# Prompt heads of a hybrid decoder step: values stationary and two heads to a product, dilated scores in pairs, no turn of the head outputs

## The chip, the cores and the metric

One core of one Trainium2 chip. The time is the device time of one execution in microseconds (us); less is better. The shapes are fixed: 256 prompt tokens, 8 sample tokens, 2 layers.

## What is computed

Each layer adds to the residual stream a mixer (latent attention, dilated-window attention and a convolution, side by side, through one output projection), and then a large expert layer (PEER). The change is in the mixer's attention over the 256 prompt tokens and in how its result reaches the output projection.

```python
for l in range(DEPTH):                                   # 2 layers
    hn = rmsnorm(xp, norm_mix[l])
    ...                                                  # project_in: queries, latents, dilated q, k, v, conv gate
    a_out = mla_prompt(q_nope, q_rope, c_kv, k_r, w_ukv[l])          # 6 heads of 64
    b_out = combine_dilations([dilated_prompt(qb, kb, vb, wdw, dl) for wdw, dl in DIL_PATTERNS], xp.dtype)  # 6 heads of 64
    c_out = conv_module(g_ext, conv_w[l], conv_b[l], conv_ln_g[l], conv_ln_b[l])                             # 256 channels
    xp = xp + jnp.concatenate([a_out, b_out, c_out], axis=-1) @ w_out[l]
    ...                                                  # PEER over 16,384 experts
```

For each head: scores of 256 queries against the keys, a mask, a softmax, and the product with the values. The 8 sample tokens have attention of their own, over 2,048 cached positions each.

## The kernel before

The kernel is written engine by engine; each engine runs its list in order, and semaphores tie them. Three of its habits matter here.

**The step loop.** After the input projection every engine walks the same loop, `for s in range(2 * NH + 2)`, 14 steps for 12 heads (0 to 5 latent, 6 to 11 dilated), L1078 for TensorE, L1447 for ScalarE, L1983 for VectorE. Head s is scored in step s (`scores`, L980: for latent heads two products of 128 and of 32 contracted rows for each half of the queries, for dilated heads one product with 64 contracted rows, L992). VectorE adds the mask, finds the maximum and writes `prob` (L1988). ScalarE takes the exponential and its sum (L1461). In step s+1 TensorE turns the three 128x128 blocks (`turn_probs`, "PT"), ScalarE copies them to `probT` (L1465). In step s+2 `mix_values` (L999, "O") takes the turned probabilities as the stationary operand and the 64 value columns as the moving one: three products of 64 columns. VectorE divides the result by the sum into `oAB`, tokens on the partitions (L2002, L2005).

Between them, in the same steps, goes the sample tokens' attention: for sequence b, in the steps of PAST_STEP = (0, 1, 2, 3, 5, 6, 8, 9), `turn_past` turns 16 + 4 blocks (banks "cT" and "rT"), which ScalarE copies out (L1454, L1456; the one `cT` buffer may be written only after sequence b-1 has been scored); one step later `score_past` ("SC", L1027, L1030), after which VectorE finds its maximum (`past_max`, L1862) and ScalarE its exponential (L1472); one step later the turn of its probabilities ("PP"), and one more the product with the cache ("ol", L1043). Steps 4 and 7 score the windows of the sample tokens ("ws", L1053), step 11 multiplies them with their values ("ow", L1073, L1075). VectorE also does the convolution: five taps in each of steps 0 to 6 (L1807), the samples' part in step 8 (L1943), its statistics in step 10 (`conv_stats`, L1954).

**Eight PSUM banks in turn.** A table of jobs, `job_plan` (L88), names every product that goes to a bank and who empties it ("V" VectorE, "A" ScalarE); job n takes bank n mod 8, and TensorE begins a job only when the bank's previous job has been emptied:

```python
PRIOR = [max([m for m in range(n) if BANK[m] == BANK[n]], default=None) for n in range(len(JOBS))]
...
if PRIOR[n] is not None:
    wait_moved(pe, *JOBS[PRIOR[n]][0])
```

So the place of a job in the table sets whom it waits for.

**The tail.** After the loop TensorE turns `oAB` to channels on partitions (L1132, "mT", six jobs of two blocks), ScalarE rounds each to a high part in `hiT` (L1514), VectorE subtracts for the low part (L2028). Then the samples' output ("os", L1137), the turn of the convolution ("ycT"), its sigmoid on ScalarE (L1517) and its product and split on VectorE (`conv_out`, L1974 to L1980). `out_high` (L1153) multiplies the high and low parts with the high part of W_out, `out_low` (L1159) the high part with its low part; of its eight blocks of rows, the last two need the convolution. ScalarE casts W_out's first half (`out_weights_high(0)`, L1509) after the loop. SyncE loads W_out's second half after the last "ol" and right behind it the first block of the query weights (L588, L669); ScalarE casts the query weights (L1523) before the second half of W_out.

## Time and profile before

| | us |
|---|---|
| median of 3 runs (2064.66 to 2067.21) | 2066.34 |
| the profiled execution, its own time | 2067.32 |
| its span, first to last instruction | 2065.4 |
| TensorE busy | 2043.7 (99%) |
| VectorE busy | 1557.4 (75%) |
| ScalarE busy | 1300.2 (63%) |
| mean DMA rate | 233 GB/s |

The span falls into two layers of about 1030 us. In each the mixer takes the first 220 us or so, the PEER layer the rest. The step loop of the second layer runs from 1115 to 1209 us. The chain that ended last is 96% TensorE, most of it the PEER products L1226 and L1273, which the change does not touch. A busy TensorE is not TensorE at its peak: weight loads that nothing hides count as busy.

### The profile page before, as it was taken

How to read it: one execution, taken by the hardware profiler on the slowest of the kernel's cores; microseconds unless marked ns; L12 is line 12 of the kernel's file. 1: busy time of each engine (PE TensorE's matmuls, PEld its weight loads, DVE VectorE, ACT ScalarE, POOL GpSimd, SP SyncE). 2: the span in 40 equal slices, each digit the busy share in tenths (PEclk: the TensorE clock that was granted, in tenths of full speed). 3: DMA queues.
4: the chain of work that ended last, by engine and by line, in shares of the span. 5: the costliest groups of instructions: out<-in, count | busy, mean ns of one | idle time of the engine just before them, and what ended most of it. 6: DMA issues, size and time to landing. Idle time of an engine off the chain costs nothing.

```text
span 2065.4 us, 40864 instructions
## 1 busy us (share of the span) xinstructions
PE 2043.7 (99%) x15610; PEld 1805.3 (87%) x15610; DVE 1557.4 (75%) x3543; ACT 1300.2 (63%) x2567; POOL 118.9 (6%) x138
## 2 busy tenths in 40 slices
PE   9999999999999999999999999999999999999998
PEld 7777899999999888788887769999999998887887
DVE  6855789868899776676677466999688997766766
ACT  5466445658888655565564564556688876655654
POOL 2200010000000010100022000000000001101000
PEclk9999999999999999999999999999999999999999
DMA  9453447776666898898763543677766668988886
GB/s 324 145 162 134 162 153 254 248 252 221 208 220 220 282 314 284 302 322 281 248 228 142 171 164 124 200 252 252 241 220 215 214 218 300 317 287 293 267 268 221
DMA packets 137377, 481.78 MB, mean 233 GB/s; under 512 B 25666, under 2 KB 42082, under 8 KB 130768
## 3 DMA queue, kind: packets, MB, share of 16 engines
q1 hardware_dynamic: 124640, 438.45, 63.6%
q0 software_dynamic: 10496, 40.42, 5.6%
q8 instruction: 126, 2.06, 0.4%
q10 hardware_dynamic: 2048, 0.30, 0.1%
q14 instruction: 67, 0.55, 0.1%
HBM read 475.83 MB, written 104.21 MB: 281 GB/s over the span
## 4 chain that ended last, share of the span: by engine, by line
PE 96%; DVE 2%; ACT 1%; DMA 1%; issue 0%; DVEq 0%; ACTq 0%
PE ps L1226 36%; PE ps L1273 33%; PE ps L842 4%; PE ps L930 3%; PE ps L1238 3%; PE ps L1189 2%; PE ps L938 2%; PE ps L1197 2%; PE ps L1193 1%; PE ps L886 1%; PE ps L1153 1%; PE ps L1027 1%; PE ps L1212 1%; PE ps L895 1%; PE ps L1030 1%; DMA big<-in_peer_wq 1%
## 5 line engine op out<-in xcount | busy, mean ns | idle before, releaser
L2220 DVE TENSOR_TENSOR parts<-region,parts 128x1024 fp32r<-128x1024 f32 x512 | 625.7, 1222 | 300.6 <-ACT parts L1548 298.3
L1226 PE MATMUL ps<-tokens_hi,parts 128*128 128x256 f32 x4096 | 760.5, 284 | 0.0
L1548 ACT CAST parts<-region 128x1024 fp32r<-128x1024 f32 x512 | 538.7, 1052 | 271.1 <-PE ps L1273 207.5
L1273 PE MATMUL ps<-parts,parts_hw 128*128 128x512 f32 x3024 | 688.7, 390 | 0.0
L1273 PEld LDWEIGHTS ps<-parts,parts_hw 128*128 128x128 f32 x3024 | 567.0, 188 | 123.8 <-DVE parts_hw L2270 6.9
L1226 PEld LDWEIGHTS ps<-tokens_hi,parts 128*128 128x128 f32 x4096 | 636.9, 188 | 1.0 <-issue 0.6
L1226 PE MATMUL ps<-parts_hw,parts 128*128 128x256 f32 x2048 | 574.1, 280 | 0.0
L1226 PEld LDWEIGHTS ps<-parts_hw,parts 128*128 128x128 f32 x2048 | 386.8, 189 | 0.0
L1594 ACT ACTIVATE big<-ps 128x256 f32<-128x256 f32 (+31 forms) x252 | 131.7, 522 | 146.9 <-PE ps L1226 146.9
L1582 ACT CAST parts_hw<-big 128x256 fp32r<-128x256 f32 x256 | 170.6, 666 | 0.7 <-DVE big L2281 0.7
L1575 ACT ACTIVATE region<-region 128x128 f16<-128x128 f16 x512 | 169.3, 436 | 0.0
L2270 DVE TENSOR_TENSOR parts_hw<-big,parts_hw 128x256 fp32r<-128x256 f32 x256 | 158.5, 619 | 6.7 <-ACT parts_hw L1582 6.7
L1238 PE MATMUL ps<-region 128*128 128x128 f16 x1024 | 81.3, 220 | 0.0
L1592 ACT ACTIVATE big<-ps 128x256 f32<-128x256 f32 (+42 forms) x130 | 36.5, 281 | 67.1 <-PE ps L1226 67.1
L811 POOL DMA_INDIRECT region<-in_peer_u,eidx x16 | 17.9, 1116 | 875.0 <-PE ps L1273 746.4
L842 PE MATMUL ps<-ident,big 128*128 128x128 f32 (+4 forms) x446 | 66.3, 277 | 0.2
L1454 ACT COPY region<-ps 128x512 f32<-128x512 f32 x64 | 32.9, 601 | 51.5 <-PE ps L1030 35.0
L1238 PEld LDWEIGHTS ps<-region 128*128 128x128 f16 x1024 | 59.0, 97 | 5.6
L842 PEld LDWEIGHTS ps<-ident,big 128*128 128x128 f32 (+4 forms) x446 | 49.8, 143 | 13.7 <-issue 10.9
L2281 DVE TENSOR_TENSOR big<-big 128x256 f32<-128x256 f32 (+42 forms) x130 | 58.5, 450 | 1.6 <-ACT big L1592 1.3
L2244 DVE TENSOR_TENSOR region<-big,region 128x512 f16<-128x512 f16 x128 | 53.4, 417 | 0.0
L2251 DVE TENSOR_TENSOR region<-region 128x512 f16<-128x512 f16 x128 | 53.4, 417 | 0.0
(328 smaller groups left out, 2244.8 us busy)
## 6 DMA issues: line engine op xcount, KB each, us to landing
region<-in_peer_uT SPq DMA_DIRECT2D x256, 512.0 KB, 4.0
region<-in_peer_v SPq DMA_DIRECT2D x256, 512.0 KB, 4.8
out<-in_state_win_k SPq DMA_DIRECT2D x112, 384.0 KB, 4.8
out<-in_state_win_v SPq DMA_DIRECT2D x112, 384.0 KB, 5.0
big<-in_window_keysT SPq DMA_DIRECT2D x16, 576.0 KB, 5.5
big<-in_state_win_v SPq DMA_DIRECT2D x48, 192.0 KB, 4.5
region<-in_w_out SPq DMA_DIRECT2D x4, 2048.0 KB, 9.0
big<-in_peer_wq SPq DMA_DIRECT2D x4, 2048.0 KB, 11.1
```

The source lines that it names most:

```text
L842: mm = pe.transpose(o[0:cols, c0:c0 + rows], src, ident[0:rows, 0:rows])
L930: mm = pe.matmul(o[t][:, 0:n], part[:, k, 128 * t:128 * t + 128], w, start=(k == 0 and i == 0), stop=False, skip_group_check=True)
L1226: mm = pe.matmul(ps[:, j % ZB, 0:SEQ], a, hp[b][:, c, :], start=(c == 0 and n == 0), stop=(c == KD - 1 and n == 2))
L1238: mm = pe.matmul(ps[:, 4 + g % GBK, 128 * k:128 * k + 128], hotA[g % 2][:, k // 2, :, k % 2], hot[g % 2][:, k // 2, :, k % 2], start=(n == ...
L1273: mm = pe.matmul(ps[:, 2 * half + t, :], w_t[a][:, 128 * t:128 * t + 128], v_t[b][:, 512 * half:512 * half + 512], start=(j == 0 and n == ...
L1548: act.copy(hi_t[n % HIGHS], rows_t[n % ROWS]).then_inc(high[l], 1)
L1575: e = act.activation(hotC[g % 2][:, k // 2, :, k % 2], place_b[g % 2][:, k // 2, :, k % 2], ACT.Copy, scale=w14[:, GG * g + k:GG * g + k + 1])
L1582: act.copy(w_parts_of(j)[0], G[:, j // JH, :, j % JH]).then_inc(w_high[now[0]], 1)
L1594: e = act.activation(G[:, j // JH, done:SEQ, j % JH], z_o[:, done:SEQ], ACT.Gelu)
L2220: dve.tensor_tensor(lo_t[n % ROWS], rows_t[n % ROWS], hi_t[n % HIGHS], ALU.subtract).then_inc(low[l], 1)
L2270: dve.tensor_tensor(w_t[1], G[:, j // JH, :, j % JH], w_t[0], ALU.subtract).then_inc(w_ready[now[0]], 1)
L2281: dve.tensor_tensor(a, a, act_t[j % 2][:, 0:done], ALU.mult).then_inc(w_mul, 1)
```

## The change

The heads are mixed in pairs. The values are now the stationary operand (64 columns of each head, head 2g into partitions 0 to 63 of the bank and head 2g+1 into 64 to 127), the turned probabilities the moving one (256 and 128 columns), so that the output has channels on its partitions and needs no turn. The division by the sum can then no longer follow the product, where the sum would lie along the free axis; VectorE divides the probabilities themselves before they are turned (`divide`), and `turn_probs` waits for that. The pair's high part is copied by ScalarE (`high_heads`) and its low part formed by VectorE (`low_heads`) in the odd steps from 3 on. Both dilated heads of a pair are scored in the even step, their products alternating between contracted rows 0 to 63 and 64 to 127. ScalarE casts W_out's first half in step 11. The bank table changes with the jobs.

```diff
@@ -85,6 +85,12 @@
 
+def scored_in(s):
+    if s < NH:
+        return [s]
+    return [s, s + 1] if s < 2 * NH and s % 2 == 0 else []
...
@@ -103,19 +109,18 @@
-        if s < 2 * NH:
-            jobs.append((("S", s), "V"))
+        jobs += [(("S", u), "V") for u in scored_in(s)]
         if s == EXT_STEP:
             jobs.append((("ext",), "V"))
         if s in PAST_STEP:
             b = PAST_STEP.index(s)
             jobs += [(("cT", b, g), "A") for g in range(4)] + [(("rT", b), "A")]
+        if s >= 3 and s % 2:
+            jobs.append((("O", (s - 3) // 2), "V"))
         if 1 <= s <= 2 * NH:
             jobs.append((("PT", s - 1), "A"))
         if s - 1 in PAST_STEP:
             jobs.append((("SC", PAST_STEP.index(s - 1)), "A"))
-        if s >= 2:
-            jobs.append((("O", s - 2), "V"))
         if s - 2 in PAST_STEP:
             jobs.append((("PP", PAST_STEP.index(s - 2)), "A"))
         if s - 3 in PAST_STEP:
@@ -134,7 +139,6 @@
-    jobs += [(("mT", g), "V") for g in range(2 * HP)]
...
@@ -152,7 +156,19 @@
-BANK = [LATE.get(name, (n if n < NUM["mT", 0] else n + 6) % 8) for n, (name, _) in enumerate(JOBS)]
+OUT_BANK = [(NUM["xo", 0, t] + 2) % 8 for t in range(2)]
+BESIDE_OUT = [b for b in range(8) if b not in OUT_BANK]
+
+
+def bank_of(n, name):
+    if name in LATE:
+        return LATE[name]
+    if NUM["PT", 2 * NH - 1] <= n < NUM["xo", 0, 0]:
+        return BESIDE_OUT[(n - NUM["PT", 2 * NH - 1]) % 6]
+    return (n if n < NUM["os",] else n + 2) % 8
+
+
+BANK = [bank_of(n, name) for n, (name, _) in enumerate(JOBS)]
 PRIOR = [max([m for m in range(n) if BANK[m] == BANK[n]], default=None) for n in range(len(JOBS))]
...
@@ -977,35 +1005,42 @@
 
-                def scores(u):
-                    o = begin("S", u)
-                    h = u % NH
+                def latent_scores(h):
+                    o = begin("S", h)
+                    r0 = 32 * (h % 4)
                     for i, c0 in ((0, 0), (1, 128)):
                         K = 128 * (i + 1)
                         qs = slice(128 * i, 128 * i + 128)
-                        if u < NH:
-                            r0 = 32 * (h % 4)
-                            pe.matmul(o[:, c0:c0 + K], qlT[:, h, qs], ckvT[:, 0:K], start=True, stop=False)
-                            mm = pe.matmul(o[:, c0:c0 + K], qrT[r0:r0 + 32, h // 4, qs], krT[r0:r0 + 32, 0:K], start=False, stop=True)
-                        else:
-                            r0 = 64 * (h % 2)
-                            mm = pe.matmul(o[:, c0:c0 + K], qbT[r0:r0 + 64, h // 2, qs], kbT[r0:r0 + 64, h // 2, 0:K], start=True, stop=True)
+                        pe.matmul(o[:, c0:c0 + K], qlT[:, h, qs], ckvT[:, 0:K], start=True, stop=False)
+                        mm = pe.matmul(o[:, c0:c0 + K], qrT[r0:r0 + 32, h // 4, qs], krT[r0:r0 + 32, 0:K], start=False, stop=True)
                     mm.then_inc(product[now[0]], 1)
 
+                def dilated_scores(g):
+                    o = [begin("S", NH + 2 * g + n) for n in range(2)]
+                    for i, c0 in ((0, 0), (1, 128)):
+                        K = 128 * (i + 1)
+                        for n in range(2):
+                            r = slice(64 * n, 64 * n + 64)
+                            mm = pe.matmul(o[n][:, c0:c0 + K], qbT[r, g, 128 * i:128 * i + 128], kbT[r, g, 0:K], start=True, stop=True)
+                            if i:
+                                mm.then_inc(product[now[0]], 1)
+
                 def turn_probs(u):
-                    pe.wait_ge(exp_ready, u + 1)
+                    pe.wait_ge(prob_ready, u + 1)
                     turn("PT", u, parts=[(prob[:, u % 2, 128 * i:128 * i + 128], 128, 128, 128 * i) for i in range(3)])
 
-                def mix_values(u):
-                    wait_moved(pe, "PT", u)
-                    if u == 0:
+                def mix_values(g):
+                    wait_moved(pe, "PT", 2 * g + 1)
+                    if g == 0:
                         wait_moved(pe, "va", 1)
-                    o = begin("O", u)
-                    v = [va[:, t, 64 * u:64 * u + 64] if u < NH else z[:, t, VB + 64 * (u - NH):VB + 64 * (u - NH) + 64] for t in range(2)]
-                    pt = probT[:, u % 2, :]
-                    pe.matmul(o[:, 0:64], pt[:, 0:128], v[0], start=True, stop=True)
-                    pe.matmul(o[:, 64:128], pt[:, 128:256], v[0], start=True, stop=False)
-                    pe.matmul(o[:, 64:128], pt[:, 256:384], v[1], start=False, stop=True).then_inc(product[now[0]], 1)
+                    o = begin("O", g)
+                    for k, (q0, q1, p0) in enumerate(((0, 256, 0), (128, 256, 256))):
+                        for n in range(2):
+                            u = 2 * g + n
+                            v = va[:, k, 64 * u:64 * u + 64] if u < NH else z[:, k, VB + 64 * (u - NH):VB + 64 * (u - NH) + 64]
+                            mm = pe.matmul(o[64 * n:64 * n + 64, q0:q1], v, probT[:, n, p0:p0 + q1 - q0], start=(k == 0), stop=(k == 1),
+                                           skip_group_check=True)
+                    mm.then_inc(product[now[0]], 1)
 
...
@@ -1075,21 +1110,33 @@
                 for s in range(2 * NH + 2):
-                    if s < 2 * NH:
-                        scores(s)
+                    if s < NH:
+                        latent_scores(s)
+                    elif scored_in(s):
+                        dilated_scores((s - NH) // 2)
                     if s == EXT_STEP:
                         o = begin("ext")
                         pe.matmul(o[0:NB, 0:48], ckvT[:, SEQ:T], qlS[:, :, 0:NH], start=True, stop=False)
                         pe.matmul(o[0:NB, 0:48], krT[0:32, SEQ:T], qrB[0:32, :, 0, :], start=False, stop=True).then_inc(product[now[0]], 1)
                     if s in PAST_STEP:
                         turn_past(PAST_STEP.index(s))
+                    if s >= 3 and s % 2:
+                        mix_values((s - 3) // 2)
                     if 1 <= s <= 2 * NH:
                         turn_probs(s - 1)
                     if s - 1 in PAST_STEP:
                         score_past(PAST_STEP.index(s - 1))
-                    if s >= 2:
-                        mix_values(s - 2)
...
@@ -1127,9 +1174,6 @@
-                wait_moved(pe, "O", 2 * NH - 1)
-                for g in range(2 * HP):
-                    turn("mT", g, parts=[(oAB[:, t, 128 * g:128 * g + 128], 128, 128, 128 * t) for t in range(2)])
...
@@ -1444,6 +1478,15 @@
+                    act.wait_ge(w_ld[now[0]][(5 + c) % 2], 16 * ((5 + c) // 2))
+                    for k in range(KD):
+                        act.copy(out_high_part(c, k), wview(5 + c)[:, k, :]).then_inc(wo_high, 1)
+
+                def high_heads(g):
+                    o = arrive(act, "O", g)
+                    act.copy(mix_hi(g), o[:, 0:SEQ]).then_inc(mix_high, 1)
+
                 for s in range(2 * NH + 2):
...
@@ -1463,6 +1506,8 @@
+                    if s >= 3 and s % 2:
+                        high_heads((s - 3) // 2)
...
@@ -1493,6 +1538,8 @@
+                        act.wait_ge(product[now[0]], NUM["S", 2 * NH - 1] + 1)
+                        out_weights_high(0)
...
@@ -1503,15 +1550,6 @@
-                def out_weights_high(c):
-                    act.wait_ge(w_ld[now[0]][(5 + c) % 2], 16 * ((5 + c) // 2))
-                    for k in range(KD):
-                        act.copy(out_high_part(c, k), wview(5 + c)[:, k, :]).then_inc(wo_high, 1)
-
-                out_weights_high(0)
-                for g in range(2 * HP):
-                    o = arrive(act, "mT", g)
-                    act.copy(hiT[:, g, 0:SEQ], o[:, 0:SEQ]).then_inc(mix_high, 1)
...
@@ -1975,14 +2013,32 @@
+                def divide(u):
+                    dve.wait_ge(exp_ready, u + 1)
+                    step(dve.reciprocal(rden[:, u, :], den[:, u, :]))
+                    settle()
+                    for i, c0 in ((0, 0), (1, 128)):
+                        pr_ = prob[:, u % 2, c0:c0 + 128 * (i + 1)]
+                        e = dve.tensor_scalar(pr_, pr_, rden[:, u, i:i + 1], None, ALU.mult)
+                    e.then_inc(prob_ready, 1)
+
+                def low_heads(g):
+                    o = read("O", g)
+                    if g == 0:
+                        dve.wait_ge(stored, 1)
+                    dve.wait_ge(mix_high, g + 1)
+                    dve.tensor_tensor(mix_lo(g), o[:, 0:SEQ], mix_hi(g), ALU.subtract).then_inc(moved_v[now[0]], 1)
 
                 for s in range(2 * NH + 2):
                     if s < 2 * NH:
                         o = read("S", s)
+                        if s >= NH and s % 2:
+                            dve.wait_ge(product[now[0]], NUM["PT", s - 2] + 1)
                         for i, c0 in ((0, 0), (1, 128)):
                             c1 = c0 + 128 * (i + 1)
                             e = dve.tensor_tensor_reduce(prob[:, s % 2, c0:c1], o[:, c0:c1], (mbias if s < NH else cbias)[:, c0:c1],
@@ -1991,19 +2047,15 @@
                         settle()
                     if s == EXT_STEP:
                         new_scores()
+                    if 1 <= s <= 2 * NH:
+                        divide(s - 1)
                     some_taps(TAPS[s] if s < len(TAPS) else 0)
                     if s - 1 in PAST_STEP:
                         past_max(PAST_STEP.index(s - 1))
                     if s == 2:
                         window_queries()
-                    u = s - 2
-                    if u >= 0:
-                        dve.wait_ge(exp_ready, u + 1)
-                        step(dve.reciprocal(rden[:, u, :], den[:, u, :]))
-                        o = read("O", u)
...
@@ -2022,10 +2074,6 @@
-                for g in range(2 * HP):
-                    o = read("mT", g)
-                    dve.wait_ge(mix_high, g + 1)
-                    dve.tensor_tensor(mix_lo[:, g, 0:SEQ], o[:, 0:SEQ], hiT[:, g, 0:SEQ], ALU.subtract).then_inc(moved_v[now[0]], 1)
```

The places where high and low parts lie change too (`mix_hi`, `mix_lo`: the high parts of the heads in the room of `oAB`, the low parts in dead columns of `z` and `va`), which is why the first `low_heads` waits for `stored`.

How the order of instructions moves, at two places. TensorE, steps 6 to 7, from the product with the cache of the sequence before on (L1043 before, L1078 now). Names: `ps` is PSUM; `region` holds the rope part and the probabilities, `ident` is the identity of a turn. Before:

```order
L1043 MATMUL ps<-big 32x128 x16
L992 MATMUL ps<-big 128x128
L992 MATMUL ps<-big 128x256
L842 MATMUL ps<-ident,region 128x128 x16
L842 MATMUL ps<-ident,big 128x128 x4
L842 MATMUL ps<-ident,region 128x128 x3
L1027 MATMUL ps<-region,big 32x512 x4
L1030 MATMUL ps<-big,region 6x128 x16
L1006 MATMUL ps<-big,region 128x64
L1007 MATMUL ps<-big,region 128x64
L1008 MATMUL ps<-big,region 128x64
L1043 MATMUL ps<-big 32x128 x16
```

And now:

```order
L1078 MATMUL ps<-big 32x128 x16
L1024 MATMUL ps<-big 128x128 x2
L1024 MATMUL ps<-big 128x256 x2
L870 MATMUL ps<-ident,region 128x128 x16
L870 MATMUL ps<-ident,big 128x128 x4
L870 MATMUL ps<-ident,region 128x128 x3
L1062 MATMUL ps<-region,big 32x512 x4
L1065 MATMUL ps<-big,region 6x128 x16
L1078 MATMUL ps<-big 32x128 x16
L870 MATMUL ps<-ident,big 128x128 x3
L870 MATMUL ps<-ident,big 8x128
L1041 MATMUL ps<-region,big 64x256 x2
```

Two heads are scored at once, and the mix of a head between "SC" and "ol" is gone; the pair's mix opens step 7. "ol" of sequence 3 stands right behind "SC" of sequence 4, and its bank was that of the scores of head 7.

VectorE, steps 10 to 11, from the end of `past_max` on (L1864 before, L1902 now); `nmx` is the negative maximum, `den` the sum. Before:

```order
L1864 TENSOR_SCALAR big<-big 128x1
L2002 RECIPROCAL rden<-den 128x2
L2005 TENSOR_TENSOR big<-ps,rden 128x2x64
L1954 BN_STATS bnst<-big 128x6
...
L1958 TENSOR_SCALAR stat<-bnst 8x1
L1988 ISA region,nmx<-ps,big 128x128
L1988 ISA nmx 128x1
L1988 ISA region,nmx<-ps,big 128x256
L1988 ISA nmx 128x1
L2002 RECIPROCAL rden<-den 128x2
L2005 TENSOR_TENSOR big<-ps,rden 128x2x64
```

And now:

```order
L1902 TENSOR_SCALAR big<-big 128x1
L1992 BN_STATS bnst<-big 128x6
...
L1996 TENSOR_SCALAR stat<-bnst 8x1
L2044 ISA region,nmx<-ps,big 128x128
L2044 ISA nmx 128x1
L2044 ISA region,nmx<-ps,big 128x256
L2044 ISA nmx 128x1
L2023 RECIPROCAL rden<-den 128x2
L2027 TENSOR_SCALAR region<-region,rden 128x128
L2027 TENSOR_SCALAR region<-region,rden 128x256
L2035 TENSOR_TENSOR big_r<-ps,big_r 128x256
```

The rows L2027 are new: the division of head 10, which its turn on TensorE waits for, stands behind `conv_stats` and the maximum of head 11.

## Rows read from the trace of the kernel before

**Rows 1.** Windows, second layer: stretch, busy us of PE, PEld, DVE, ACT, POOL; then clock, DMA, GB/s.

```profile
1115.00:1243.00 128.00, 123.57 (x1414) 90.20 (x1413) 73.54 (x226) 76.03 (x195) 3.91 (x4) 1.00 0.45 153
```

**Rows 2.** Waits of TensorE, 1115 to 1245 us: us in total, times, longest.

```profile
PE ps L1153 <- DVE big_r L1980: 1.8, 1, 1.8
...
PE ps L992 <- ACT region L1465: 0.8, 1, 0.8
```

**Rows 3.** Timeline of TensorE, second layer: start us, us, instruction, [idle before].

```profile
1127.92 2.40 PE L842 MATMUL ps<-ident,big 128*128 128x128 f32 x20
...
1182.86 1.06 PE L1027 MATMUL ps<-region,big 128*32 128x512 f32 x8
...
1184.73 0.43 PE L1006 MATMUL ps<-big,region 128*128 128x64 f32 x2
...
1185.65 1.08 PE L1043 MATMUL ps<-region,big 128*32 128x128 f32 x32
...
1188.75 0.92 PE L992 MATMUL ps<-big 64*128 64x128 f32 x4 [0.78 <-ACT region L1465]
1189.60 0.55 PE L842 MATMUL ps<-ident,region 128*128 128x128 f32 x3
...
1196.91 2.14 PE L1073 MATMUL ps<-big 128*32 128x384 f32 x24
1198.99 0.91 PE L1075 MATMUL ps<-big 8*128 8x384 f32 x2
...
1208.78 1.75 PE L842 MATMUL ps<-ident,big 128*128 128x128 f32 x12
...
1217.05 0.47 PE L1153 MATMUL ps<-big_r,tokens_hi 128*128 128x512 f32 x1 [1.75 <-DVE big_r L1980]
...
1225.61 3.68 PE L895 MATMUL ps<-region,big 128*8 128x128 f32 x128
```

**Rows 4.** Groups by shape, TensorE, 1099 to 1115.1 us: count, busy us, mean ns, idle.

```profile
L886 PE MATMUL ps<-big 128*128 128x288 f32 x16 | 4.2, 413 | 0.7 <-DMA big<-in_w_ukT 0.7
...
L886 PE MATMUL ps<-big 64*128 64x264 f32 x12 | 1.6, 400 | 0.0
```

**Rows 5.** Timeline of VectorE, second layer.

```profile
1173.94 0.56 DVE L1883 COPY big<-ps 128x384 f32<-128x384 f32 x1 [2.11 <-PE ps L1057]
...
1175.38 0.28 DVE L1988 CUSTOM_DVE_ANT_0 region<-ps,big 128x128 f32<-128x128 f32 x1
...
1178.21 0.41 DVE L1943 TENSOR_TENSOR region<-region 128x248 f32<-128x248 f32 x1
...
1180.55 0.29 DVE L1988 CUSTOM_DVE_ANT_0 region<-ps,big 128x128 f32<-128x128 f32 x1 [0.18 <-DVE region L1947]
...
1193.42 0.42 DVE L1954 BATCH_NORM_STATS2 bnst<-big 128x6 f32<-128x256 f32 x1
...
1195.87 0.29 DVE L1988 CUSTOM_DVE_ANT_0 region<-ps,big 128x128 f32<-128x128 f32 x1 [0.18 <-DVE stat L1958]
...
1196.42 0.16 DVE L2002 RECIPROCAL rden<-den 128x2 f32<-128x2 f32 x1
...
1206.48 1.05 DVE L1967 TENSOR_SCALAR big<-big,bnst,stat 128x256 f32<-128x256 f32 x3
...
1209.99 2.08 DVE L2028 TENSOR_TENSOR big_r<-ps,tokens_hi 128x256 fp32r<-128x256 f32 x6 [0.83 <-ACT tokens_hi L1514]
```

**Rows 6.** Timeline of ScalarE, second layer.

```profile
1184.92 2.05 ACT L1454 COPY region<-ps 128x512 f32<-128x512 f32 x4 [4.56 <-PE ps L1030]
...
1188.20 0.50 ACT L1465 COPY region<-ps 128x384 f32<-128x384 f32 x1
...
1211.28 1.28 ACT L1517 ACT_TABLE_LOAD   x1
```

**Rows 7.** Chain of waits, 1030 to 1300 us: start us, us, what.

```profile
1205.39 14.15 DMA big<-in_peer_wq
```

**Rows 8.** Windows, first layer, columns as in rows 1.

```profile
182.00:194.00 12.00, 12.00 (x59) 9.77 (x58) 7.95 (x22) 7.36 (x15) 0.00 (x0) 0.57 0.92 342
```

More of the change, by code:

```diff
@@ L1076, in mix_window, with out_high @@
                               skip_group_check=True).then_inc(product[now[0]], 1)
+                def out_high(c, t, k0, k1):
+                    o = begin("xo", c, t) if k0 == 0 else bank("xo", c, t)
+                    for k in range(k0, k1):
+                        pe.wait_ge(wo_high, KD * c + k + 1)
+                        if c == 0 and k == 2 * HP:
+                            wait_moved(pe, "ycT", 1)
+                        for i, part in enumerate((mix_hi(k), mix_lo(k))):
+                            pe.matmul(o[:, 0:512], part[:, 128 * t:128 * t + 128], out_high_part(c, k), start=(k == 0 and i == 0), stop=False,
+                                      skip_group_check=True)
                 for s in range(2 * NH + 2):
-                    if s < 2 * NH:
-                        scores(s)
+                    if s < NH:
+                        latent_scores(s)
+                    elif scored_in(s):
+                        dilated_scores((s - NH) // 2)
                     if s == EXT_STEP:
@@ L1142, in _ @@
                     turn("ycT", c, parts=tokens(yt, 128 * c))
-                wait_moved(pe, "mT", 5)
                 wait_moved(pe, "os")
-                def out_high(c, t):
-                    o = begin("xo", c, t)
-                    for k in range(KD):
-                        pe.wait_ge(wo_high, KD * c + k + 1)
-                        if c == 0 and k == 2 * HP:
-                            wait_moved(pe, "ycT", 1)
-                        for i, part in enumerate((hiT, mix_lo)):
-                            pe.matmul(o[:, 0:512], part[:, k, 128 * t:128 * t + 128], out_high_part(c, k), start=(k == 0 and i == 0), stop=False,
-                                      skip_group_check=True)
+                wait_moved(pe, "O", 2 * HP - 1)
                 def out_low(c, t):
@@ L1998, in _ @@
                         window_queries()
[L1999 to L2006 removed]
+                    if s >= 3 and s % 2:
+                        low_heads((s - 3) // 2)
                     if s in WINDOW_STEP:
```

31 lines of the change are left out of this document (19 added, 12 removed).

## The prediction, made before the changed kernel ran

> **What bounds the kernel now.** I read the page's chain first: 96% TensorE, nearly all of it PEER, which stays as it is. So only the mixer counts, some 125 us of each layer. Then the windows over it: TensorE is busy 123.57 of 128 us, VectorE 73.54 and ScalarE 76.03 [rows 1]. In the step loop TensorE leads and the others keep up; its waits there are 0.8 us on ScalarE in step 10, and 1.8 us in the tail for the convolution's low part [rows 2]. Work taken off TensorE in the loop is therefore worth its full time, but only as long as the two other engines deliver in time: each of them is idle because TensorE is late, and their chains have latencies which a shorter TensorE step uncovers. So I price the work first and then look for every place where TensorE would arrive early. Times are those of the second layer; the first has the same sequence. T is the end of the sample scores "SC" of sequence 6, 1184.73 us [rows 3].
>
> **TensorE's work.** Mix: a head takes 0.92 us from its start to the next instruction (1184.73 to 1185.65) [rows 3]; over the 12 heads these spans run from 0.61 to 0.92 and add up to 9.2. Now a pair has 256 + 128 moving columns for each head, in two column halves. If the halves run side by side, that is 384 columns. A product of 288 columns on all rows takes 4.2/8 = 0.52 us, so 384 take 0.69; that column strips do run side by side is seen in the window mix, where 12 products of 384 columns in four strips need 2.08 us, 0.17 each [rows 3, 4]. With entry and exit I take 0.9 for a pair (ends 0.7 and, not side by side, 1.5): 9.2 - 5.4 = **3.8 saved**. Dilated scores: a head takes 0.85 (1188.75 to 1189.60) [rows 3]. Products with 64 contracted rows that alternate between the row halves are there already: six of 264 columns in 1.6 us, 0.27 each, where one on all rows takes 0.52 for 288 [rows 4]. So a pair costs about what a head did, 0.9 (ends 0.8 and 1.7): 5.1 - 2.7 = **2.4 saved**. The turns "mT" go: **1.7 saved** [rows 3]. Together 7.9 us of each layer.
>
> **VectorE's work.** The division of 128 outputs becomes one of 384 probabilities. Nearest row: a tensor by scalar of 256 elements, 0.35 us (three in 1.05); with the reciprocal's 0.27 and 0.1 to 0.2 for the 128-element part, **0.7 us a head** [rows 5]. Over the loop it adds little to an engine that idles 40% of the time. What it changes is the order: the division of head s-1 stands behind the maximum of head s (0.6 us, 1195.87 to 1196.42 and a little [rows 5]), and TensorE's turn PT(s-1) waits for it. Before, that turn needed ScalarE alone. In steps that open with 2.4 us of past turns (20 blocks, [rows 3]) this is hidden; in the others it is not.
>
> **Where TensorE now waits, up to T.** (a) "ol" of step 3 takes the bank of cT(3,1), which ScalarE empties 1.1 us after "SC"; "PP" covers 0.5: 0.6. (b) Step 4 has no past turns: from the end of S(4) VectorE needs 0.6 for the maximum, 0.7 for the new token's scores and 0.7 to divide, TensorE has one small product: 1.9 until PT(3). (c) Step 6: "ol" now has the bank of S(7), and VectorE comes to S(7) only after the maximum of "SC" (0.9), a small reciprocal (0.2) and 0.6 of its own; TensorE has nothing between: 1.8. (d) Step 8: "ol" has the bank of S(9). From the end of the window scores VectorE needs 1.4 (window maximum), 0.6, 0.7, 2.3 (samples' convolution) and 0.6 = 5.6; TensorE 0.9 + 2.4 + 0.4 + 0.5 = 4.2: 1.4, say 1.5 [rows 5, 3]. Sum 5.8. Up to T seven heads become four pairs (5.4 to 3.6) and four dilated heads two pairs (3.4 to 1.8): -3.4. **T comes 2.4 us later.**
>
> **From T to the window mix**, before 12.2 us (1184.73 to 1196.91 [rows 3]). S(10) now has the bank of O(3), the pair that was just mixed. ScalarE empties the four "cT", "rT", takes an exponential and copies PT(8), until T+4.0 (1188.70 [rows 6]), then the high part, and VectorE the low part, 0.35 each (2.08/6 [rows 5]): S(10) starts at T+4.8, where TensorE is ready at 3.0. The pair ends at 5.7, maximum and division at 7.1, PT(9) 7.6, "SC" (1.87) 9.5. Then VectorE takes its maximum (10.4), **`conv_stats`, 2.4 us** (12.8), the maximum of head 11 and the division of head 10: 14.1. TensorE has mixed a pair meanwhile and waits 3 us, the longest new wait. PT(10), "PP", "ol" (1.0) and one turn: 16.3. **4.1 us later.**
>
> **From there to the output projection's second part** (before 20.1 us, 1196.91 to 1217.05). Two single mixes (1.5) become a pair (0.9), behind 0.3 of wait: ScalarE's eight casts of W_out, 4.3 us, now stand ahead of the copies of the window mix, but the mix of the second group covers them except for 1 us, and TensorE has PT(11) and "ol" then. Without "mT" 1.7 go, less 0.3 which the copy for "os" then shows. ScalarE's table load before the sigmoid (1.28 us from 1211.28 [rows 6]) no longer stands behind "mT": 1.0. **2.7 us earlier.** From here on all is as before: `out_low` ends 8.6 us later (1225.61 [rows 3]).
>
> Off the path: the query weights' transfer is issued behind the last "ol" and lands after 14.15 us [rows 7]. "ol" ends at T+23.5 instead of T+20, so the weights land at T+38; ScalarE's casts (3.9 + 4.3) end at 46.3, VectorE gets there at 47.6. It stays hidden by 1.3 us; one more microsecond of delay would show. `stored` is set long before step 3 (the stores land in 10 us, some 15 us earlier).
>
> **Sum.** +2.4 + 4.1 - 2.7 = +3.8 us a layer, 7.6 for both. The profiled execution took 2067.3, 1.0 above the median of the runs: 2066.3 + 7.6 = **2074 us**. Differences of less than 0.2%, 4.1 us, count as none.
>
> The Trainium skill, TensorEngine Tiling (Array Packing), section Key Properties, says that a change of the tiling mode drains the array. The mixes had the same mode as the turns around them and now have another.
>
> **The rivals.** *Full gain, faster (0.12).* VectorE's divisions are ready when TensorE comes; the place is PT(10): the theory holds if the turn starts before T+11, which it would if VectorE took S(11), there since T+5.7, ahead of the statistics. The order rows say it doesn't. Then only the bank waits (c) and (d), 3.3 us, stand against 7.9 + 1.0: -5.6 a layer, 2055 us. *Balance (0.22).* The waits, 12.7 us a layer in my sum (3.8 + 7.9 + 1.0), are a third smaller, since each is a difference of two chains, and TensorE's work just pays for them: 2066 us. *Drain (0.08).* Each change of mode costs some 0.2 us: a dilated head's 384 columns take 0.85 where the rate of rows 4 gives 0.69. Two changes at each of four pairs on the path: +1.6 a layer, 2077 us; the rule named above says the same in kind. *No overlap (0.08).* The halves run one after the other: 0.6 for each of some five mixes and 0.8 for each of three score pairs, +5.4 a layer, 2085 us. It speaks against it that both kinds of overlap are in rows 3 and 4, though the column halves only as strips of 32. *Clock (0.10).* In the first layer the clock falls to 1.2 GHz in the tail, 0.57 on average over 12 us [rows 8], after a stretch of products of a few columns; the second layer keeps 1.00 [rows 1]. New idle stretches of 2 to 3 us just before the tail could bring it down in both: ten microseconds at half speed, between 0 and 5 us, so 2077 us. My forecast has 0.40.
>
> **Numbers.** Slower by over 0.2%: 0.40 + 0.10 + 0.08 + 0.08 = 0.66; within 0.2%: 0.22; faster: 0.12. The range leaves out the full gain and the upper half of no overlap: 2062 to 2083 us.
>
> **What would show it.** L1024 in pairs at 0.9 us and L1041 at 0.9 a pair; waits of TensorE on VectorE before PT(3) of 1.9 us, before L1078 in steps 6 and 8 of 1.5 to 1.8, before S(10) of 1.8 and before PT(10) of 3; no "mT", and the span from the last window mix to L1120 shorter. I am wrong if TensorE's waits in the second layer's loop add up to less than 8 us, or if L1041 takes 1.5 us a pair.

## The result, and the profile after

The changed kernel took 2088.27 us (median of 6 runs, 2083.20 to 2090.41), the kernel before 2066.78 (6 runs): ratio 1.0103, 95% interval 1.0090 to 1.0116. That is slower, as forecast, by 21.5 us instead of 7.6, and outside the range of 2062 to 2083.

The profiled execution has a span of 2086.1 us, 20.7 more than before. The page's summary and its chain of waits still show TensorE busy nearly always:

```profile
PE 2039.9 (98%) x15538; PEld 1793.4 (86%) x15538; DVE 1564.7 (75%) x3567; ACT 1302.5 (62%) x2567; POOL 119.9 (6%) x138
...
PE 94%; DVE 3%; ACT 2%; issue 1%; DMA 0%; DVEq 0%; ACTq 0%
```

From the first latent score of head 0 to the end of `out_low` the second layer's mixer takes 121.9 us (1124.36 to 1246.29), before 110.6 (1115.00 to 1225.61, the end in [rows 3]); the first layer's 122.6, before 112.7. The stretch between the two mixers is unchanged (912.2 us, 912.3 before). So everything lies where the prediction looked, +9.9 us in the first layer and +11.3 in the second. The waits of TensorE there, 1110 to 1260 us (engine, line, whom it waited for, us in total, times, longest):

```profile
PE ps L870 <- DVE region L2027: 5.8, 3, 2.6
PE ps L1078 <- ACT region L1497: 2.6, 2, 1.7
PE ps L1078 <- DVE nmx L2044: 2.0, 1, 2.0
PE ps L1024 <- DVE big_r L2035: 1.6, 1, 1.6
PE ps L870 <- ACT region L1497: 0.9, 1, 0.9
PE ps L1041 <- ACT region L1508: 0.6, 1, 0.6
PE ps L1181 <- DVE big L2070: 0.3, 1, 0.3
PE ps L1014 <- ACT region L1497: 0.2, 1, 0.2
```

14.0 us, where the kernel before had 3.0 (0.8 and 1.8 of [rows 2] and two of 0.2). The timeline of TensorE shows them in their places:

```profile
1147.35 0.87 PE L1041 MATMUL ps<-region,big 128*64 128x256 f32 x8
1148.15 0.55 PE L870 MATMUL ps<-ident,region 128*128 128x128 f32 x3
...
1149.51 1.06 PE L1065 MATMUL ps<-big,region 128*6 128x128 f32 x32
1151.42 0.63 PE L870 MATMUL ps<-ident,big 128*128 128x128 f32 x4 [0.85 <-ACT region L1497]
...
1157.22 0.55 PE L870 MATMUL ps<-ident,region 128*128 128x128 f32 x3 [1.72 <-DVE region L2027]
...
1158.74 1.95 PE L1065 MATMUL ps<-big,region 128*6 128x128 f32 x32
...
1171.97 0.93 PE L1024 MATMUL ps<-big 64*128 64x128 f32 x8
1172.83 1.97 PE L870 MATMUL ps<-ident,region 128*128 128x128 f32 x16
...
1179.13 1.08 PE L1078 MATMUL ps<-big 128*32 128x128 f32 x32 [1.70 <-ACT region L1497]
...
1181.39 0.87 PE L1041 MATMUL ps<-region,big 128*64 128x256 f32 x8 [0.59 <-ACT region L1508]
...
1193.39 1.08 PE L1078 MATMUL ps<-region,big 128*32 128x128 f32 x32 [2.00 <-DVE nmx L2044]
...
1204.71 0.93 PE L1024 MATMUL ps<-big 64*128 64x128 f32 x8 [1.59 <-DVE big_r L2035]
1207.03 0.90 PE L870 MATMUL ps<-ident,region 128*128 128x128 f32 x3 [1.39 <-DVE region L2027]
...
1209.57 1.94 PE L1065 MATMUL ps<-big,region 128*6 128x128 f32 x32
...
1216.24 0.76 PE L870 MATMUL ps<-ident,region 128*128 128x128 f32 x3 [2.64 <-DVE region L2027]
```

A pair's mix takes 0.80 us to the next instruction (1147.35 to 1148.15) and a pair's scores 0.86 (1171.97 to 1172.83). The waits stand before PT(3), "ol" of steps 6 and 8, S(10), PT(9) and PT(10). The one at 1179.13 is put down to ScalarE, but it is the bank of S(7): VectorE finished with it at 1178.98, and e7 below, which frees that bank sooner, takes the wait away.

What the prediction did not have is in the duration column. The same 32 products (L1065) take 1.06 us at 1149.51 and 1.94 or 1.95 at 1158.74 and 1209.57. The windows name the reason (columns as in [rows 1]):

```profile
1124.00:1220.00 96.00, 82.47 (x999) 55.84 (x997) 47.14 (x174) 53.83 (x149) 3.96 (x4) 0.93 0.41 140
1220.00:1247.00 27.00, 26.61 (x234) 18.51 (x236) 15.01 (x41) 15.85 (x28) 0.00 (x0) 0.94 0.43 157
1155.00:1165.00 10.00, 8.28 (x133) 4.80 (x133) 4.88 (x17) 4.07 (x13) 2.76 (x3) 0.83 0.56 175
1205.00:1215.00 10.00, 7.21 (x63) 3.52 (x61) 4.21 (x19) 4.23 (x14) 0.00 (x0) 0.66 0.42 161
1215.00:1225.00 10.00, 8.76 (x91) 4.33 (x91) 4.70 (x22) 6.51 (x17) 0.00 (x0) 0.83 0.00 0
```

The granted clock goes from 2.4 to 1.2 GHz four times, from about 1158.4, 1206.2, 1216.4 and 1233.5 us on. A mean of 0.93 over 96 us with two levels, 1 and 0.5, is 13.7 us at the lower one (from the unrounded value), and the tail adds 3.4: 17.1 us in the second layer's mixer, where the kernel before had none [rows 1], and 17.1 in the first, where it had 10.2 [rows 8]. In this layer the falls in the loop come behind PT(3), between S(10) and PT(9), and behind PT(10); in the first they come behind "ol" of step 8, between S(10) and PT(9), and behind PT(10). Not every long wait has one: 1.70 and 2.00 us before "ol" of steps 6 and 8 passed at full clock in this layer, and so did the wait before PT(3) (1.75 us) in the first.

What it costs can be read by laying the same sequence at both levels side by side. From the turn PT to the end of "PP" it takes 2.9 us at full clock (1182.19 to 1185.12), 4.5 from 1157.22 and 5.5 from 1207.03: 1.5 and, with the mix behind the latter, 2.8 us more. PT(10) to the window mix takes 3.8 (1216.24 to 1220.04) against 2.2 in the next section's e2 (1194.26 to 1196.50), and the first twelve products of the output projection 4.4 (1233.38 to 1237.82) against 2.9 (e2, 1227.21 to 1230.10). Together the instructions are 7.4 us longer.

Not all of that is on the path. PT(10) waits for VectorE and starts 4.8 us behind the end of "SC" in both layers. In the first, "PP" and the mix between them ran at full clock, and the wait is longer instead:

```profile
180.97 0.55 PE L870 MATMUL ps<-ident,region 128*128 128x128 f32 x3 [3.37 <-DVE region L2027]
```

So 0.7 us of the 7.4 only took the place of idle time (3.37 against 2.64). The same goes for the tail. The second part of the output projection needs the convolution's low part, which VectorE finishes at 1237.30:

```profile
1233.38 4.61 PE L1120 MATMUL ps<-big_r 128*128 128x512 f32 x12
1237.82 0.40 PE L1120 MATMUL ps<-big_r,tokens_hi 128*128 128x512 f32 x1
```

```profile
1236.87 0.43 DVE L2018 TENSOR_TENSOR big_r<-big,tokens_hi 128x256 fp32r<-128x256 f32 x1
```

At full clock TensorE would have been there at 1236.3 and waited until about 1237.45 (in the kernel before and in e6 it starts 0.15 us behind VectorE). That hides 1.2 us more. The lower clock thus cost the second layer about **5.5 us**. The same reading of the first layer gives 6.2 us (1.7 at the turns behind "ol" of step 8, 1.4 at PT(9), 1.6 at PT(10), 1.5 in the tail); the kernel before had lost 2.0 there, the whole difference between its two mixers, which are alike until the clock falls. That is 4.1 more, and **9.6 us** for both layers. These are estimates, worked out from the timelines of both layers in the two traces.

### The profile page after: what moved, and what is told of

It reads as the page before. It is cut to its first block, busy times and chain, and to the rows that moved or that the text cites. A ratio compares the mean times of both kernels' runs of the same rounds, so it can differ in the third digit from the quotient of the medians.

```text
span 2086.1 us, 40721 instructions
## 1 busy us (share of the span) xinstructions
PE 2039.9 (98%) x15538; PEld 1793.4 (86%) x15538; DVE 1564.7 (75%) x3567; ACT 1302.5 (62%) x2567; POOL 119.9 (6%) x138
## 4 chain that ended last, share of the span: by engine, by line
PE 94%; DVE 3%; ACT 2%; issue 1%; DMA 0%; DVEq 0%; ACTq 0%
PE ps L1260 35%; PE ps L1307 33%; PE ps L870 3%; PE ps L958 3%; PE ps L1272 3%; PE ps L1223 2%; PE ps L966 2%; PE ps L1231 1%; PE ps L1227 1%; PE ps L1120 1%; PE ps L914 1%; PE ps L1062 1%; PE ps L1065 1%; PE ps L1246 1%; PE ps L923 1%; PE ps L1193 1%
## 5 line engine op out<-in xcount | busy, mean ns | idle before, releaser
L870 PE MATMUL ps<-ident,big 128*128 128x128 f32 (+2 forms) x422 | 63.8, 279 | 1.7 <-ACT region L1497 1.7
L870 PEld LDWEIGHTS ps<-ident,big 128*128 128x128 f32 (+2 forms) x422 | 46.8, 141 | 17.5 <-issue 15.0
```

The source lines that it names most:

```text
L870: mm = pe.transpose(o[0:cols, c0:c0 + rows], src, ident[0:rows, 0:rows])
```

## The experiments

Each changes the changed kernel, unless it says otherwise. "Granted clock" and waits are of the second layer's mixer, from each run's one profile. TensorE's products in the fills are turns of the identity that nobody reads.

**e1: fills in three waits.**

```diff
 def turn_probs(u):
+    if u in FILL:                       # {3: 14, 9: 11, 10: 21}
+        o = begin("PT", u)
+        for _ in range(FILL[u]): pe.transpose(o[:, 384:512], ident, ident)
     pe.wait_ge(prob_ready, u + 1)
```

> The change, with products that nobody reads put into three of TensorE's waits: 14 turns of 128 columns before the turn of head 3's probabilities, 11 before head 9's and 21 before head 10's, each about as long as the wait. No wait is removed and no other engine does anything else. Theory A (idle stretches of 1.4 to 2.6 us are what the clock fell after): in the second layer the falls to 0.5 right behind PT(3) and PT(10) are gone, which gives back 1.9 and 1.6 us, and the same in the first layer: 2088 becomes 2081, or about 2074 if the other falls go too. Rival B (the clock falls because pairs leave TensorE with less work in a step, or because of the other tiling): the falls stay where they are and the time is 2088 or a little more.

Measured 2081.4 us (5 runs), ratio to before 1.0064 (1.0050 to 1.0078): theory A's number. No work or delay was removed, and 7 us went (6.0 in the profiled executions, 5.0 of them in the two mixers). Windows of the second layer:

```profile
1150.00:1160.00 10.00, 9.95 (x153) 6.47 (x151) 6.00 (x21) 3.84 (x13) 2.54 (x3) 1.00 0.70 224
1185.00:1195.00 10.00, 8.22 (x103) 6.49 (x103) 1.90 (x10) 2.33 (x9) 0.00 (x0) 0.83 0.30 108
```

The fall behind PT(3) is gone, and so are those around PT(9) and PT(10); a new one stands behind the wait of 2.0 us before "ol" of step 8, which was not filled. The first layer went from 17.1 to 6.8 us at the lower level and lost 4.2 us; in the second the tail has 10.2 us of it, so only 0.8 us were won there.

**e3: the division first. e4: the statistics later. e7: both maxima of a pair together.** Three single moves on VectorE:

```diff
 for s in range(2 * NH + 2):             # e3
+    if 1 <= s <= 2 * NH: divide(s - 1)
     if s < 2 * NH: ... maximum of S(s)
-    if 1 <= s <= 2 * NH: divide(s - 1)

-CONV_STEP = (8, 9, 10, 11, 12)          # e4
+CONV_STEP = (8, 9, 11, 11, 12)

-    if s < 2 * NH: ... maximum of S(s)  # e7
+    if s < NH or s in range(NH, 2 * NH, 2): reduce_scores(s)
     ...
     divide(s - 1)
+    if s in range(NH, 2 * NH, 2): reduce_scores(s + 1)
```

> The change with one thing moved: VectorE divides head s-1 before it takes the maximum of head s. Theory A: the waits before PT(3) (1.7 us) and PT(9) (1.4) go, with the clock's fall in step 4 (1.9): some 5 us a layer, 2078. Rival C: the division waits for ScalarE's exponential, the maximum behind it comes later, and the time stays at 2088 within 2 us.

> The change with one thing moved: the convolution's statistics (2.4 us of VectorE) from step 10 to step 11, behind the division of head 10. Theory A: the wait before PT(10) falls from 2.6 to under 0.5 us, and the clock's fall behind it (1.6 us) goes: some 4 us a layer, 2080. Rival D (it is the chain maximum, exponential, division that PT(10) waits for, with or without the statistics): the wait stays over 2 us, and the time at 2088.

> The change with one thing moved: VectorE takes the maximum of the second head of a dilated pair in the pair's first step, behind the division there, and not in the next step. Theory A: the waits before ol(3) (1.7 us) and ol(4) (2.0), which stand for the banks of S(7) and S(9), go, and that before PT(10) falls by 0.7; some of it returns before the third pair's mix, which waits for ScalarE: 2 to 4 us a layer, 2080 to 2084. Rival (the chain through ScalarE's cT copies sets the step, the banks do not): 2088.

e3: 2088.65 us, no change; rival C was right. The wait before PT(3) fell to 0.5 and that before PT(9) went, but "ol" of step 6 now waits three times as long. TensorE, VectorE and ScalarE:

```profile
1179.39 1.94 PE L1078 MATMUL ps<-big 128*32 128x128 f32 x32 [5.02 <-DVE nmx L2046]
```

```profile
1177.94 0.17 DVE L2023 RECIPROCAL rden<-den 128x2 f32<-128x2 f32 x1 [2.55 <-ACT region L1504]
```

```profile
1174.50 2.05 ACT L1497 COPY region<-ps 128x512 f32<-128x512 f32 x4 [4.56 <-PE ps L1065]
1176.41 0.63 ACT L1499 COPY big<-ps 128x512 f32<-128x512 f32 x1
1176.89 0.44 ACT L1504 ACTIVATE region<-region,nmx 128x128 f32<-128x128 f32 x1
```

Read from below: ScalarE idles 4.56 us for the past scores, copies cT and rT, and only then takes the exponentials; the division waits for them, the maximum of S(7) for the division, and "ol" for the bank of S(7).

e4: 2081.2 us, ratio 1.0074 (1.0061 to 1.0088), 1.2 us over the expected 2080: PT(10) waits 0.9 in place of 2.6 (not under 0.5), and both layers have 3.4 us less at the lower clock.

e7: 2087.7 us, no gain, where 2080 to 2084 stood. The wait for the bank of S(7) is gone and that for S(9) is 0.5, but the pair's mix behind waits 2.47 instead of 0.59 for ScalarE's copy of PT(5), which stands behind the same cT copies; the lower clock lasts 41 us in and just ahead of the two mixers, against 34. Of the three single moves, e3 and e7 shifted the wait to the next link of a chain; only e4 gained.

**e2 and e5: the orders together.** e2 has e3, e4 and e7, and ScalarE takes a pair's high part ahead of cT. e5 adds:

```diff
-    exponentials(s); copy_probs(s - 1)  # ScalarE, steps with past turns
+    copy_probs(s - 1); exponentials(s)
+    divide(11) ahead of conv_stats()    # VectorE, step 11
```

> The change with the orders of VectorE and ScalarE rearranged and TensorE's untouched: the division of head s-1 ahead of the maximum of head s, both maxima of a dilated pair in its first step, the convolution's statistics one step later, the high part of a pair ahead of ScalarE's cT copies. Theory A: the 13.8 us of waits in the second layer's loop fall below 4 us, the clock stays at 1.00 there, and the saved 7.9 us of TensorE work a layer show: 2050 to 2060 us, less than before the change. Rival B: the waits go, some 10 us a layer, but the clock falls as often as in the changed kernel: 2066 to 2070. Rival C (the divisions wait for the exponentials and hold up the maxima behind them): new waits of the same size, 2080 or more.

> The rearranged kernel of e2_order with two more moves: in the steps with past turns ScalarE copies the turned probabilities ahead of the next exponentials, and VectorE divides head 11 ahead of the convolution's statistics. Theory A: the wait before the third pair's mix, 2.5 us in e2_order, falls to about 1.4, those before S(10) (0.9) and PT(11) (0.9) go, and the clock's fall behind the mix goes too: 2.9 us less idle and 1.6 less at half clock in each layer, 2060 to 2063 us, faster than before the change. Rival B (the falls of the clock do not hang on the waits): 2063 to 2069 with as many falls.

e2: 2068.9 us, ratio 1.0011 (1.0002 to 1.0020). Nineteen of the 21.5 us are back, by order alone, but theory A had promised 2050 to 2060. Its waits are 7.3 us, not under 4, the largest 2.47 before the third pair's mix with a fall of the clock behind it. The lower clock lasts 6.8 us in each mixer instead of 17.1. A further fall of 3.4 us stands in the input projection, just ahead of the second layer's loop, where TensorE waits nowhere more than 0.4 us; the 16 products there take 4.74 us, in the changed kernel 3.09:

```profile
1108.39 4.74 PE L914 MATMUL ps<-big 64*128 64x264 f32 x16
```

The profile is of the fastest of the eleven executions (2065.2 us), so a usual one may have more. e5: 2067.0 us, ratio 1.0002 (0.9993 to 1.0011), the time of the kernel before and 4 us over the expectation: the mix waits 1.62, but PT(6) now waits 0.78 and PT(9) 0.63, since the exponentials came later, and the clock still falls behind the mix. I had priced what the move took away and not what it put in.

**e9, e10, e11: exponentials in ScalarE's idle time.** e9 takes back e5's swap and moves the exponentials ahead of the cT copies, into the idle 4.56 us above. e10 also moves the turn of the last probabilities ahead of the past turns in steps 6 and 8, e11 in step 6 alone.

```diff
+    exponentials(s)                     # ScalarE, e9
     if s in PAST_STEP: cT and rT copies
-    exponentials(s)

+PT_FIRST = (6, 8)                       # e10; (6,) in e11
+    if s in PT_FIRST: turn_probs(s - 1) # the same in the list of jobs and on ScalarE
     if s in PAST_STEP: turn_past(...)
```

> As e5_order2, but ScalarE takes the exponentials of head s before it copies that step's cT (which wait for the last sample's scores while ScalarE idles 3 to 4 us), and not behind the turned probabilities; PT and cT keep their order. Theory A: the divisions never wait, so the waits before PT(6), PT(9) and PT(10) in e5_order2 (1.8 us) go and the one before the third pair's mix stays at 1.6, where the copy of PT(5) still stands behind cT: 2060 to 2064. If the waits don't move the time (rival B: only the falls of the clock do, and they come as before), 2067.

> e9_exp_first with the turn of head s-1's probabilities and its copy ahead of the past turns in steps 6 and 8. Theory A: ScalarE has PT(5) copied before the pair's mix needs it, the last wait over 1 us in the loop is gone and the clock stays at 1.00 from the first head to the window mix in both layers; waits in the loop about 3 us: 2054 to 2060, clearly faster than before the change. Rival B: the clock still falls once or twice a layer within the loop, with no wait over 1 us ahead of the fall, and the time is over 2061.

> e10_probs_first with the turn put ahead in step 6 alone: in step 8 it waited 1.5 us for the division of head 7, which comes later than TensorE there. Theory A: that wait goes, 0.5 us of wait for the bank of S(9) come back in step 8: 1 us a layer, 2057. If the second window's or the past's chain sets step 8 anyway: 2059.

e9: 2062.6 us, ratio 0.9978 (0.9969 to 0.9987). e10: 2059.1, ratio 0.9963 (0.9950 to 0.9977). e11: **2056.6 us**, ratio 0.9957 (0.9944 to 0.9971), all three as expected (e10, too, has 1.00 through both loops); e11 is 9.9 us faster than the kernel before and 32 faster than the change, with the change's products. Its windows, first and second layer, loop and tail:

```profile
89.00:176.00 87.00, 83.00 (x1087) 56.15 (x1087) 49.44 (x187) 59.24 (x160) 3.91 (x4) 1.00 0.46 154
176.00:197.00 21.00, 20.50 (x142) 16.23 (x145) 11.89 (x27) 10.33 (x17) 0.00 (x0) 0.84 0.56 201
1108.00:1197.00 89.00, 84.79 (x1115) 57.46 (x1115) 50.26 (x191) 60.85 (x164) 3.91 (x4) 1.00 0.45 153
1197.00:1215.00 18.00, 17.70 (x116) 14.15 (x116) 11.29 (x24) 8.29 (x12) 0.00 (x0) 0.91 0.64 233
```

No wait in the loop is over 1.0 us and the clock stays up there in both layers; in the tail it still falls.

**e13 and e14: the waits without the pairs.** So far every kernel with added waits had the pairs too. These two are the kernel before.

```diff
+HELD = {3: (3, 15), 10: (4, 21)}        # VectorE operations, fills
     pe.wait_ge(exp_ready, u + 1)
+    if u in HELD:
+        o = begin("PT", u)
+        for _ in range(HELD[u][1]): pe.transpose(o[:, 384:512], ident, ident)   # e14 only
+        pe.wait_ge(held, ...)           # set by VectorE behind HELD[u][0] operations
```

> The kernel before the change, without pairs, with TensorE held back twice in each layer's loop: the turn of head 3's probabilities waits some 1.9 us and that of head 10's some 2.7 us for a signal that VectorE gives after a few operations whose results nobody reads. Theory A (idle stretches bring the clock down): the second layer, whose clock stays at 1.00 in the kernel before, shows a fall to 0.5 behind one or both of the waits; 4.6 us of waiting and 1.5 to 3.5 at half clock a layer, 2079 to 2083. Rival B (the pairs are what brings it down): no fall in the loop, 2074 to 2077.

> e13_before_held with 15 and 21 products of 128 columns, which nobody reads, in the time in which TensorE is held back. The same delay, without an idle stretch. Theory A: no fall in the loop of either layer, 2074 to 2077, 3 to 7 us under e13_before_held. Rival (it is the delay of what follows, or an effect of the other engines' extra work, not TensorE's idleness): the same time as e13_before_held.

e13: 2091.4 us, ratio 1.0118 (1.0103 to 1.0134). e14: 2082.0, ratio 1.0082 (1.0069 to 1.0096). Both are over their numbers because the waits came out at 2.5 and 5.0 us, not 1.9 and 2.7: the signal stood behind VectorE's other work in step 11. What they were made for is between them. Of e13, the two waits and the windows behind them:

```profile
1158.18 0.52 PE L844 MATMUL ps<-ident,region 128*128 128x128 f32 x3 [2.52 <-DVEq L2003]
...
1213.55 0.87 PE L844 MATMUL ps<-ident,region 128*128 128x128 f32 x3 [5.03 <-DVEq L2003]
```

```profile
1158.00:1168.00 10.00, 9.82 (x140) 6.38 (x140) 4.89 (x14) 2.01 (x5) 0.68 (x1) 0.83 0.41 122
1209.00:1219.00 10.00, 5.45 (x59) 4.26 (x63) 4.84 (x20) 2.57 (x8) 0.00 (x0) 0.66 0.01 2
```

and of e14, the loop and the tail:

```profile
1119.00:1211.00 92.00, 87.93 (x1081) 63.94 (x1080) 47.26 (x174) 52.66 (x145) 4.10 (x4) 1.00 0.44 149
1211.00:1239.00 28.00, 27.97 (x232) 20.98 (x236) 15.29 (x40) 19.58 (x35) 0.00 (x0) 0.88 0.43 151
```

Without a single pair the clock falls behind each added wait, in both layers, and with products in the first 1.9 and 2.5 us of the same waits it stays at 1.00 through both loops of e14's profiled execution, though 0.5 and 2.4 us of idle time are left:

```profile
1201.02 2.51 PE L1002 MATMUL ps<-ident 128*128 128x128 f32 x21
1205.92 0.55 PE L844 MATMUL ps<-ident,region 128*128 128x128 f32 x3 [2.39 <-DVEq L2005]
```

PT(3) comes 32.95 us behind the first score in e13 and 32.75 in e14, so the delay is the same; 9.3 us lie between the two times. Two of e14's five executions took 2085.8 and 2085.9 us with a mean clock of 0.993 over the whole (0.996 to 0.997 in the three others): in those the clock was lower for longer, at places that no profile shows. The other half of the comparison is e11: all the pairs, no wait over 1.0 us, and no fall in either loop.

**e6, e8, e12: fills in the tail**, where TensorE has products of 4 to 8 columns. There are 8 turns ahead of `olT` and 4 ahead of `os` (two products of the samples' output) in e6 (on e5) and e8 (on the kernel before), 4 and 4 in e12 (on e11).

> e5_order2 with 8 products of 128 columns put ahead of the product olT and 4 ahead of os, where TensorE otherwise has only products of 4 to 8 columns; nobody reads them. They cost 1.4 us of TensorE a layer. If the clock's fall in the tail, at the first part of the output projection, comes behind a stretch of such small products, it goes, which gives back up to 1.7 us a layer: the same time as e5_order2 within 2 us, with one fall less in each layer. If the fall has another cause it stays, and the time is 3 us above e5_order2.

> The kernel before the change with the same 12 products that nobody reads, ahead of olT and os. In the first layer its clock is at 0.5 for 10.2 us from 183 us on. If that fall comes behind the stretch of small products, it goes: it gives back some 2 to 5 us and the products cost 2.8 in both layers together, so 2064 to 2068. If not, 2070.

> e11_probs_first_6 with 4 products of 128 columns ahead of olT and 4 ahead of os, which nobody reads (0.9 us of TensorE a layer). In e10_probs_first the clock was at 0.5 for 6.8 us in each layer's tail and nowhere else in the mixer. If the few products are enough to keep it up, up to 3.4 us a layer come back less 0.9, but the second part of the output projection then waits for the convolution's low part, some 1 us as in e6_tail_fill: 2054 to 2057. If they are not enough, or the convolution's part sets the tail's end: 2057 to 2059.

e6: 2067.3 us, as e5. Both tails are at full clock, where e5's have 6.8 us each at the lower one, and nothing is won: the fills take 1.4 us and the second part of the output projection then waits for the convolution's low part:

```profile
1197.00:1226.00 29.00, 27.25 (x251) 18.53 (x242) 17.00 (x51) 18.29 (x35) 0.00 (x0) 1.00 0.40 146
```

```profile
1217.15 0.47 PE L1120 MATMUL ps<-big_r,tokens_hi 128*128 128x512 f32 x1 [1.02 <-DVE big_r L2028]
```

e8: 2069.1 us, 2.0 above the kernel before (1.0014, 1.0005 to 1.0023), outside 2064 to 2068 and 1 us short of 2070: in its profile the first layer's tail has 3.4 us at the lower level instead of 10.2, and the second's 10.2 instead of none. e12: 2060.9, 4.3 above e11 and outside both ranges; four and four did not hold the clock (6.8 us at the lower level in each tail, where e11 has 6.8 and 3.4). So small products are not shown to be what the tail's falls come from, and what decides them stays open.

## Why the prediction was wrong

**The work: right for a pair.** Pairs were put at 0.9 us and take 0.80 and 0.86. The drain of the tiling mode, a rival at 0.2 us for each change, is not seen: over the 0.69 us of its columns a pair has 0.1 to 0.2 us in all. The Trainium skill's rule that a change of mode drains the array (TensorEngine Tiling (Array Packing), Key Properties) can cost no more than that here. No overlap (1.5) is refuted by the same rows. In all, the second layer's +11.3 us are 11.0 of wait and 7.4 of longer instructions less 7.1 of work saved, where 7.9 stood; the difference lies ahead of T (2.5 saved, 3.4 forecast), and I have not put it to single instructions.

**The waits: right in place and nearly in size.** PT(3): 1.9 forecast, 1.72 measured. "ol" of step 6: 1.8 and 1.70; of step 8: 1.5 and 2.00. S(10): 1.8 and 1.59, starting at T+4.8 as forecast. PT(9): 1.4 and 1.39. PT(10): 3 and 2.64. The first cT bank: 0.6 and 0.85, one job earlier, at "PP". Not foreseen were the same bank wait at "ol" behind T (0.85) and the mix behind ScalarE's copy of PT(5) (0.59). Forecast were 12.7 us a layer, less 1.0 in the tail, 11.7 in all. The waits grew by 14.0 - 3.0 = 11.0, and by 12.9 with the 1.9 us that the lower clock covered.

**The sum: 2 us a layer too low even without the clock.** T came 5.8 us late, of which 1.5 are clock; from T to the window mix it took 8.0 more, 3.6 of them clock; from there to the second part of the output projection 2.4 less, in spite of 0.4 for the clock. Without the clock that is +4.3, +4.4 and -2.7, against +2.4, +4.1 and -2.7. Of the second layer's 11.3 us 5.5 are clock and 5.8 are left, where the sum had 3.8: 1.2 more of wait and 0.8 less of work saved. The first layer, read by itself, gives 9.9 - 4.1 = 5.8 too. With these 11.6 us alone the time would have been 2078, inside the range.

**The step that failed is the clock rival**: "ten microseconds at half speed, between 0 and 5 us", at 0.10 and as an alternative to the forecast, with a fall just before the tail. It is no alternative: it is a term that the forecast's own waits bring with them. There are four falls a layer, three of them in the loop, with 34 us at the lower level in both mixers where the kernel before had 10. They cost 5.5 + 4.1 = 9.6 us where 0 to 5 stood. The tail, where the rival looked for the fall, is where it costs least: 0.4 us in the second layer. The row was in hand: TensorE's idle time was to rise from 3 to 14 us in 122, in stretches of up to 3 us, and nothing in the trace of a kernel without such stretches said that they were free. e1, e11, e13 and e14 show the cause of the falls in the loop: the idle stretches, not the pairs. What sets which wait has a fall behind it stays open. The hidden transfer of the query weights stayed hidden, landing at T+41.6 (38 forecast).

## What to carry to other kernels

When a change shortens the leading engine's work and leaves the other engines' chains as they are, price the waits that appear, and then a second time for the clock: here 11 us of new idle time a layer brought 4 to 6 more. Where a wait can't be removed, products that nobody reads can be tried in its place (e1: 7 us for 46 of them a layer), but look for the link of the chain first. Much of it was one queue here, ScalarE's, where an exponential stood behind copies that waited for something else; moving it into that queue's idle time (e5 to e9, with e5's own swap taken back) gave 4.3 us. The orders together turned 21.5 us of loss into 10 of gain, while two of the three single moves (e3, e7) only handed the wait on.

## What the runs showed of the hardware

Some stretches of 1.6 to 2.6 us without a product were followed by a granted clock of 0.5, in a kernel with pairs (1.72, 1.59 with 1.39 behind it, 2.64 us) and in one without (2.52 us in e13). It isn't one rule for each wait: 1.70 and 2.00 us passed without a fall in the changed kernel's second layer, 1.75 in its first, and in e9 a wait of 1.62 us stands before the third pair's mix in both layers, with a fall behind it in the second layer (0.83 over 1160 to 1170 us) and none in the first (1.00 over 91 to 180). TensorE: Matmul & The Clock Gate, in the Trainium skill, section "A second HAM failure mode: psum-queue depth-cycling", tells of a kernel whose frequent short idle times between groups of products make the clock go to and fro; e13 against e14 agrees in kind, with 2.5 us of idle time for the shorter wait.

Nor does every fall stand behind a wait. In the profiles of e2, e5, e6, e7, e8 and e9 the clock also falls for 3.4 us at a time in the input projection of one layer, with no wait of TensorE over 1.0 us in the 15 us before it, and every kernel but e6 has a fall in one tail or both. No run here settles what brings these.
